# Feed-forward of a two-layer backbone on one core: up and gate tiles in four groups (6, 6, 6, 4) in place of three (8, 8, 6)

## The reference

```
def _conv_ffn(h, w_up, conv_w, conv_b, w_down):
    u = h @ w_up                                   # 1024 -> 2 * 2816
    u = lax.conv_general_dilated(u, conv_w[:, None, :], window_strides=(1,), padding=[(1, 1)], ...) + conv_b
    a, g = jnp.split(u, 2, axis=-1)
    return (jax.nn.silu(a) * g) @ w_down           # 2816 -> 1024

x = x + g2 * _conv_ffn(h2, ffn_w_up[i], ffn_conv_w[i], ffn_conv_b[i], ffn_w_down[i])
```

## Time and profile before

| what | value |
|---|---|
| median of 3 runs | 2088.53 us |
| profiled execution, its own time | 2089.09 us |
| its span | 2086.8 us |
| granted clock of PE, mean | 0.98 |
| PE busy | 1987.6 us (95%) |
| DVE busy | 1342.7 us (64%) |
| ACT busy | 755.7 us (36%) |
| read from HBM | 181.15 MB, 89 GB/s over the span |

### The profile page before, as it was taken

How to read it: one execution, slowest core, us unless ns; L and a number is a source line. 1 busy time by engine, 2 the same in 40 slices (tenths; PEclk the granted TensorE clock), 3 DMA queues, 4 the chain that set the end, 5 groups by cost and what they waited for, 6 DMA issues and landing times.

```text
span 2086.8 us, 29934 instructions
## 1 busy us (share of the span) xinstructions
PE 1987.6 (95%) x10452; PEld 1691.5 (81%) x10452; DVE 1342.7 (64%) x2251; ACT 755.7 (36%) x1281; POOL 97.4 (5%) x162
## 2 busy tenths in 40 slices
PE   5999999999999899999999998899999789999997
PEld 4878888888888778888888887788888668888785
DVE  7866645735745687756664666878778557557375
ACT  5423223223223344312321333556656335333232
POOL 0000000000000000000000000311110000000000
PEclk9999999999999999999999999999999889999999
DMA  7221311321221112243233224211111222222222
GB/s 290 81 91 61 111 61 52 110 66 59 91 81 61 61 61 90 91 141 102 100 106 127 99 90 151 91 49 56 45 40 50 71 71 90 93 98 98 94 90 101
DMA packets 51255, 186.37 MB, mean 89 GB/s; under 512 B 5680, under 2 KB 5680, under 8 KB 51184
## 3 DMA queue, kind: packets, MB, share of 16 engines
q1 hardware_dynamic: 37744, 136.73, 19.5%
q0 software_dynamic: 13440, 48.63, 7.1%
HBM read 181.15 MB, written 4.19 MB: 89 GB/s over the span
## 4 chain that ended last, share of the span: by engine, by line
PE 83%; DVE 9%; issue 4%; ACT 3%; DMA 1%; DVEq 0%; SPq 0%; ACTq 0%
PE acc L390 59%; PE o_ps L480 3%; PE o_ps L515 3%; PE acc L603 3%; PE acc L480 2%; PE o_ps L646 2%; PE acc L661 2%; PE acc L502 2%; PE acc L445 2%; DVE pt_lo L1612 1%; PE o_ps L661 1%; PE acc L636 1%; PE o_ps L431 1%; DVE w_lo L1156 1%; ACT w_hi L793 1%
## 5 line engine op out<-in xcount | busy, mean ns | idle before, releaser
L793 ACT ACTIVATE w_hi<-raw 128x1024 fp32r<-128x1024 f32 x232 | 245.1, 1057 | 609.1 <-PE acc L390 500.8
L1156 DVE TENSOR_TENSOR w_lo<-raw,w_hi 128x1024 fp32r<-128x1024 f32 x232 | 284.1, 1225 | 274.4 <-ACT w_hi L793 272.9
L390 PE MATMUL acc<-h_hi,w_hi 128*128 128x512 f32 x1520 | 436.2, 350 | 5.4 <-DVE w_lo L1156 3.4
L390 PE MATMUL acc<-h_hi,w_lo 128*128 128x512 f32 x1520 | 436.4, 350 | 0.0
L390 PE MATMUL acc<-h_lo,w_hi 128*128 128x512 f32 x1520 | 434.3, 349 | 0.0
L390 PEld LDWEIGHTS acc<-h_hi,w_hi 128*128 128x128 f32 x1520 | 245.7, 189 | 46.2 <-ACT u L979 4.1
L390 PEld LDWEIGHTS acc<-h_lo,w_hi 128*128 128x128 f32 x1520 | 244.0, 188 | 39.1
L390 PEld LDWEIGHTS acc<-h_hi,w_lo 128*128 128x128 f32 x1520 | 244.5, 188 | 38.3
L1323 DVE SCALAR_TENSOR_TENSOR x<-acc,mod,x 128x512 f32<-128x512 f32 (+3 forms) x136 | 81.9, 636 | 145.1 <-PE acc L390 135.8
L390 PE MATMUL acc<-act_hi,w_hi 128*128 128x512 f32 (+1 forms) x396 | 119.9, 357 | 0.0
L390 PE MATMUL acc<-act_lo,w_hi 128*128 128x512 f32 (+1 forms) x396 | 119.4, 355 | 0.0
(11 more groups left out here) (230 smaller groups left out, 3529.7 us busy)
## 6 DMA issues: line engine op xcount, KB each, us to landing
raw<-in_weights_dram SPq DMA_DIRECT2D x232, 512.0 KB, 3.3
ada_raw<-in_ada_dram POOLq DMA_DIRECT2D x80, 512.0 KB, 3.6
ada_start<-in_ada_first_dram SPq DMA_DIRECT2D x8, 1024.0 KB, 18.3
x<-in_x_in_dram SPq DMA_DIRECT2D x4, 768.0 KB, 6.9
park_dram<-x POOLq DMA_DIRECT2D x1, 2048.0 KB, 8.1
rel<-in_bias_dram POOLq DMA_DIRECT2D x16, 128.0 KB, 2.5
out_dram<-x SPq DMA_DIRECT2D x8, 256.0 KB, 2.2
x<-park_dram POOLq DMA_DIRECT2D x1, 1536.0 KB, 9.2
```

What stands on the lines that cost most here:

```text
L390: mm = nc.tensor.matmul(tile[:, c0:c0 + cn], wt[:, b * P:(b + 1) * P], mv[:, n, c0:c0 + cn], start=(n == 0 and m == 0), stop=(n == last an ...
L793: nc.scalar.activation(w_hi[i][:, :], raw[i][:, :], ACT.Copy).then_inc(hi_split, 1)
L1156: nc.vector.tensor_tensor(w_lo[i][:, :], raw[i][:, :], w_hi[i][:, :].bitcast(F32), ALU.subtract)\
```

## The change

The three groups of 8, 8 and 6 blocks become four of 6, 6, 6 and 4, in both layers. `act_hi` and `act_lo` have room for six blocks instead of eight. There are eight more down chunks in each layer, since every group loads eight, padded to full size. The sum over hidden blocks is the same, and so is the number of matmuls. The rows of `ada_w[1]` are spread anew: per group 6, 6, 6, 4 in the up pairs, 2 at each group's D0 and D1, and 6, 6, 6, 0 in the later down tiles (before: 8, 8, 6, then 3, 3, 2, then 6, 6, 6), 48 in all. The step with both conditions stood in the first group (17 rows) and stands in the first two (28 rows) now.

```
-GROUPS = (8, 8, 6)
-UP_ADA, FIRST_ADA, DOWN_ADA = (1, 1, 1), (3, 3, 2), (2, 2, 2)
+GROUPS = (6, 6, 6, 4)
+UP_ADA, FIRST_ADA, DOWN_ADA = (1, 1, 1, 1), (2, 2, 2, 2), (2, 2, 2, 0)
...
-                act_hi = sb("act_hi", [P, 8, TOK], F32R, part)
-                act_lo = sb("act_lo", [P, 8, TOK], F32R, part)
+                act_hi = sb("act_hi", [P, max(GROUPS), TOK], F32R, part)
+                act_lo = sb("act_lo", [P, max(GROUPS), TOK], F32R, part)
...
-                    conds = 2 if n == 0 else 1
+                    conds = 2 if n < 2 else 1
...
-                    pairs = 2 if ends and n == 2 else 3
                     last = n == len(GROUPS) - 1
+                    pairs = 2 if ends and last else 3
```

## The result

| what | before | after |
|---|---|---|
| median of 4 runs, side by side | 2087.85 us (2086.13 to 2088.62) | 2104.57 us (2099.99 to 2107.03) |
| ratio, 95% interval | | 1.0080 (1.0062 to 1.0098) |
| profiled execution, its own time | 2089.09 us | 2107.03 us |
| its span | 2086.8 us | 2105.1 us |
| granted clock, mean | 0.98 | 0.978 |

The account below looks back on a forecast made before the run. PE was taken as the bound. Layer 0 (5.7 + 2.7 + 0.4 = 8.8) and layer 1 (6.3 + 1.2 + 0.4 + 1.2 = 9.1) add 17.9 us to 2089.09; less 0.56, 2106.5 us, 8-in-10 range 2100 to 2112.

Parts of the forecast that it names:

- PE is the bound, and only its idle time counts: In both feed-forwards PE hardly waits, so the change can add or remove time only where PE stands still.
- the sum: Whole kernel: 8.8 us added in layer 0 and 9.1 in layer 1, together 17.9; forecast chance 55%.
- The waits for `act_lo`: At group ends, a fixed latency less the blocks PE can do meanwhile: 5.7 us added in layer 0, 6.3 in layer 1.
- the 0.1 of each restart: After each wait of PE, the first matmul costs 0.1 us more.
- D2 and D3 behind the groups of 4: After the last group's restart PE waits for w_lo: 2.7 us at D2 and D3 in layer 0, 1.2 at layer 1's D2.
- D3 in the groups with both conditions: Layer 0's two such groups: D3's w_lo comes 11.8 us after act_lo, PE waits some 0.2 each, 0.4 in all.
- The loop of the last group in layer 1: A raw buffer's turn of 5.7 us against 5.6 for two tiles: 0.4 us, between 0 and 1.5.
- The clock: Granted clock falls behind the waits of the groups of 4: free in layer 0, 1.2 us in layer 1.
- more than the sum: Rival, 22%: clock falls behind layer 1's 1.9 us waits too (up to 5 us, 2111.5), or ada_step ring reaches PE (2113).
- the ring that reaches PE: Down loops with both conditions: an ada_step turn of 6.7 us against 6.3 a tile would add up to 6.4 us.
- only the waits for `act_lo`: Rival, 18%: D2's and D3's weights come in time and the clock stays, leaving 12.0 us, so 2100.5.
- not slower: Rival, 3%: new buffer addresses speed PE's matmuls in both layers by 18.4 us, taking back the loss: 2088.

Follow-up runs that it names:

- e7_conds: The changed kernel with the steps beside the second group's down tiles done for the latents' condition alone, up pairs keeping both; 2104.46 us, ratio 1.0088 to the kernel before.
- e2_layer1: The kernel before with layer 1 alone in four groups (6, 6, 6, 4), layer 0 still 8, 8, 6; 2097.13 us, ratio 1.0052.
- e10_small_first: The changed kernel with its group sizes in the order 4, 6, 6, 6; 2119.67 us, ratio 1.0150 to the kernel before.
- e3_act8: The changed kernel with act_hi and act_lo back at eight blocks, restoring the old addresses; 2103.14 us, ratio 1.0085 to the kernel before.
- e4_notap_after: The changed kernel without the convolution's middle tap, one DVE pass between up tile and act_lo; 2097.63 us, ratio 1.0060 to the kernel before.
- e5: The kernel before without the convolution's middle tap, one DVE pass between up tile and act_lo; 2083.37 us, ratio 0.9986.
- e6_cover: The changed kernel with all but the last of D1's blocks, instead of two, ahead of the wait for act_lo; 2105.30 us, ratio 1.0096 to the kernel before.
- e8: The kernel before with the split of each up pair's second chunk moved later, in both layers; 2085.64 us, ratio 0.9997.
- e1_layer0: The kernel before with layer 0 alone in four groups (6, 6, 6, 4), layer 1 still 8, 8, 6; 2095.02 us, ratio 1.0048.
- e11_877: The kernel before with groups of 8, 7 and 7 in place of 8, 8 and 6; 2085.71 us, ratio 0.9997.
- e12_877_late: The kernel before with groups of 8, 7 and 7 and, in layer 1, a later split of each up pair's second chunk; 2084.90 us, ratio 0.9994.

## Why the prediction was right, and where a size was off

- **PE is the bound, and only its idle time counts.** Held. No wait of PE beyond those of the sum goes with DVE's 48 us, the 8 MB more chunks and the longer ring in two groups, and e7_conds, which takes out eight passes of 1.22 us, wins 0.2 us of layer 0 by it.
- **The waits for `act_lo`.** Forecast 1.0, 1.0, 1.0 and 3.0 in layer 0 and 1.9, 1.9, 1.9 and 3.3 in layer 1. Measured 0.9, 0.9, 0.9, 3.0 and 1.9, 1.9, 1.9, 2.7 (with 0.3 at D1's chunk just ahead). Latency less cover is right to 0.3 us at each. By the starts, with the 0.1 of each restart, it is 5.6 us more than before in layer 0 and, with the 0.3 at D1, 6.3 in layer 1; the sum had 5.7 and 6.3. What I had missed is the third chunk of this place, D1's, and it cost nothing of its own.
- **D2 and D3 behind the groups of 4.** The listed waits are 1.35 and 0.93 in layer 0 and 1.09 in layer 1. By the starts PE is late by 1.51 and 1.09 and by 1.25, each with 0.1 behind it: 2.8 us where the sum had 2.7, and 1.35 where it had 1.2. D3's weight came when it should (1280.46 - 1270.30 = 10.2 us after the restart, forecast 10.1).
- **D3 in the groups with both conditions.** The term of 0.4 is there, though the list of waits doesn't show it, since the gaps are too short for it. In after's first group (it answers to the earlier trace rows) D3's `w_lo` ends at 859.22 + 1.22 = 860.44, 11.8 us after `act_lo` (848.67), as forecast. D2 starts at 854.09, 5.37 us after D0's restart at 848.72; five blocks and 0.1 are 5.35. So D3 was due at 854.09 + 6.30 = 860.39, just ahead of its weight. DVE's split, and PE from the end of D2 on:

```profile
859.22 1.22 DVE L1156 TENSOR_TENSOR w_lo<-raw,w_hi 128x1024 fp32r<-128x1024 f32 x1
```
```profile
860.04 0.51 PE L390 MATMUL acc<-act_hi,w_lo 128*128 128x512 f32 x2
860.56 0.61 PE L390 MATMUL acc<-act_hi,w_hi 128*128 128x512 f32 x2
861.01 0.52 PE L390 MATMUL acc<-act_lo,w_hi 128*128 128x512 f32 x2
```

The starts are 0.52 and 0.45 us apart where 0.35 is the rule: 0.27 lost here, and 0.2 in the second group (1011.77, 1012.23, 1012.68), 0.5 for the 0.4 of the sum. A restart costs 0.10 us at each of these places, the 0.1 of the sum. With 5.6 and 2.8 the down tiles of layer 0 lose 8.9 us; 9.0 are measured and 8.8 were forecast. Its feed-forward is only 8.3 longer, because the up tiles of its first group take 0.6 less, which the sum didn't have.
- **The loop of the last group in layer 1.** Forecast 0.4, measured 0.2 in after and about 1.0 in e2_layer1. A turn of 5.7 us stands against 5.6, so either was possible.
- **The clock.** This is the step that failed: the place of the fall was wrong, and that its size came out near is luck. I expected the fall behind the waits of about 3 us. In after these were followed by full clock, and the fall stands behind the third wait of 1.9 us in layer 1. Stretches of after (the columns as above):

```profile
1989.00:1993.00 4.00, 4.00 (x12) 3.14 (x11) 1.98 (x2) 1.03 (x1) 0.00 (x0) 0.57 0.15 19
1993.00:1996.00 3.00, 3.00 (x15) 2.41 (x14) 1.98 (x2) 1.06 (x1) 0.00 (x0) 1.00 0.38 149
...
2069.00:2072.00 3.00, 2.20 (x9) 1.43 (x9) 2.40 (x3) 2.17 (x3) 0.00 (x0) 1.00 0.00 0
```

That one fall costs 4.00 x 0.43 = 1.7 us, against the 1.2 that the sum had for a fall behind the last boundary. The rival "more than the sum" had this mechanism right and its number of falls too high: one, not three. Its other half, the ring that reaches PE, came true only in e10_small_first, where it was given no slack. There the falls came at all four boundaries of layer 1, so its "more falls" was not far off either.
- **The sum.** Layer 0 8.3 us for 8.8, layer 1 9.4 for 9.1. The spans differ by 18.3, the medians by 16.7; the sum said 17.9. The profiled execution of after is the longest of its four, 2.5 us over their median, so the agreement within 0.4 us with its span is closer than the runs can bear out. The rival "only the waits for `act_lo`" is out by 3.4 us of waits for `w_lo` at D2 and D3 that stand in the rows, and "not slower" by e3_act8.

The four runs of after lie between 2099.99 and 2107.03 us. That is no wider than before's, whose 23 runs beside e4, e5, e6 and e8 lie between 2082.68 and 2090.15.

## What to carry to other kernels

Where a loop is cut into groups, each cut costs what is left of a fixed latency when the work that the bounding engine can lay over it has run out; write down both for the smallest group before choosing sizes. Count all latencies that stand in a row there: moving work from under the second to under the first gains nothing (e6_cover), and only a larger group or a shorter chain does. Put the smallest group where there is least side work beside it (e10_small_first: 15 us by the medians, 7.7 of it net of the clock in layer 0), and expect work that another engine gains off the path to be nearly free as long as what PE waits for doesn't stand behind it (e7_conds: eight passes, 0.2 us).

## What the hardware showed that I had not expected

- A wait of about 1.9 us can be followed by the lower clock or not, in the same place of the same code. In after, e2_layer1, e3_act8 and e7_conds there are twelve such waits at layer 1's boundaries. Four were followed by a fall, one in each execution: behind the second in e3_act8, the third in the others. The four waits of 2.7 us that follow were not followed by one. In e10_small_first all four were, the one of 2.7 and the three of 1.9. Of the waits of 3.0 us in layer 0, after, e1_layer0 and e3_act8 show no fall behind them, e7_conds and e10_small_first one. A longer wait isn't a surer fall; what decides isn't settled by these runs.
- The up tiles of layer 0's first group run at one of two paces. Granted clock 1.00 and no wait throughout, and PE starts so many matmuls in 100 us (stretch, its us, PE busy and count, clock, DMA share, GB/s), in before, e11_877 and e12_877_late:

```profile
770.00:870.00 100.00, 100.00 (x567) 1.00 0.30 97
```
```profile
770.00:870.00 100.00, 100.00 (x578) 1.00 0.30 100
```
```profile
770.00:870.00 100.00, 100.00 (x568) 1.00 0.29 96
```

  A product of 768 columns (two matmuls) starts every 0.3534 us or every 0.3467. The slow pace is that of twelve of the fourteen kernels, the fast one that of e4_notap_after and e11_877. In the second group all are fast but e10_small_first, and later all. It explains three differences that lie in no wait. Of the 2.2 us between e11_877 and e12_877_late in layer 0, 2.0 are there (556.55 and 558.78 us net, with the same code in that layer). So are the 1.4 us of e4_notap_after, and the 0.6 us that layer 0's up tiles take less in after, whose first group has six blocks and not eight. What sets the pace isn't known. With one trace for each kernel I can't say either whether it goes with the kernel or with the execution. It is a warning against reading 2 us out of one pair of traces.
